# A new order of the work, a wider norm, a block placing moved to ScalarE and a last product moved to GpSimd in a two-layer hybrid model

## The reference

```python
def rms_norm(x, g):
    y = x * lax.rsqrt(jnp.mean(x * x, axis=-1, keepdims=True) + EPS)
    return y * g

for l in range(2):
    h = rms_norm(x, norm_mix_g[l])
    pa, pb, pc, pg = jnp.split(h @ w_in[l], GROUP_POINTS, axis=-1)
    oa = rwkv7_time_mix(pa, ...)          # S = S * w - (S kk)(kk a)^T + v k^T ; o = S r, token by token
    ob = stick_breaking_attention(pb)
    oc = differential_attention(pc, ...)
    ga, gb, gc = jnp.split(sigmoid(pg), 3, axis=-1)
    x = x + (ga * (oa @ w_branch_a[l]) + gb * (ob @ w_branch_b[l]) + gc * (oc @ w_branch_c[l])) @ w_out[l]
    x = x + conv_ffn(rms_norm(x, norm_ffn_g[l]), ...)
return rms_norm(x, norm_final_g)
```

## Time and profile before

| what | value |
|---|---|
| median of 3 runs | 1030.68 us (1030.68, 1030.68, 1032.37) |
| the profiled execution | 1032.37 us, of which the span is 1030.5 us and 1.9 us lie around it |
| PE, DVE, ACT, POOL busy | 98%, 80%, 60%, 1% |
| mean granted clock of TensorE | 0.997 |
| HBM | 157 GB/s, DMA engines 45% busy |

### The profile page before, as it was taken

How to read it: one execution, slowest core, us unless ns; L and a number is a source line. 1 busy time by engine, 2 the same in 40 slices (tenths; PEclk the granted TensorE clock), 3 DMA queues, 4 the chain that set the end, 5 groups by cost and what they waited for, 6 DMA issues and landing times.

```text
span 1030.5 us, 22708 instructions
## 1 busy us (share of the span) xinstructions
PE 1012.3 (98%) x8522; PEld 945.8 (92%) x8522; DVE 819.7 (80%) x1371; ACT 618.6 (60%) x967; POOL 11.9 (1%) x30
## 2 busy tenths in 40 slices
PE   8999999999999999999999999999999999999997
PEld 7998988899999999999999989789999999999996
DVE  6799763797797898878778996649968789887876
ACT  7964332656556665766689533246656666666765
POOL 0000000100000000000000000010000000000000
PEclk9999999999999999999999999999999999999999
DMA  8452342335445565555534533233435445555553
GB/s 300 156 173 103 116 150 64 114 111 177 156 157 182 181 206 184 185 190 180 197 131 155 175 111 135 83 90 126 148 141 184 165 164 204 193 192 190 184 185 126
DMA packets 46282, 163.93 MB, mean 159 GB/s; under 512 B 5904, under 2 KB 6080, under 8 KB 46192
## 3 DMA queue, kind: packets, MB, share of 16 engines
q1 hardware_dynamic: 44640, 160.19, 45.0%
q10 hardware_dynamic: 864, 1.63, 0.6%
q0 software_dynamic: 688, 0.81, 0.4%
HBM read 161.04 MB, written 1.05 MB: 157 GB/s over the span
## 4 chain that ended last, share of the span: by engine, by line
PE 85%; DVE 9%; ACT 3%; issue 2%; DMA 1%; SPq 0%; DVEq 0%; ACTq 0%
PE psum L468 84%; DVE sb_lo L1306 2%; ACT sb_rw L916 1%; DMA sb_raw<-w_stream 1%; DVE sb_inv L1555 1%; DVE sb_inv L1514 1%; DVE sb_inv L1517 1%; PE psum L786 1%; ACT sb_hh L916 1%; ACT sb_hi L916 0%; DVE sb_rw L1598 0%; DVE sb_yf L1579 0%; DVE sb_qb L1364 0%; DVE sb_rw L1485 0%; DVE sb_inv L1491 0%
## 5 line engine op out<-in xcount | busy, mean ns | idle before, releaser
L916 ACT ACTIVATE sb_hi<-sb_raw 128x1024 fp32r<-128x1024 f32 (+1 forms) x298 | 310.2, 1052 | 168.6 <-PE psum L468 158.6
L1306 DVE TENSOR_TENSOR sb_lo<-sb_raw,sb_hi 128x1024 fp32r<-128x1024 f32 x296 | 357.9, 1218 | 53.3 <-ACT sb_hi L916 52.9
L468 PE MATMUL psum<-sb_hh,sb_hi 128*128 128x256 f32 x1184 | 344.3, 291 | 2.6 <-DVE sb_lo L1306 1.3
L468 PE MATMUL psum<-sb_o,sb_hi 128*128 128x256 f32 (+1 forms) x1728 | 339.6, 308 | 1.3 <-DVE sb_o L1327 1.3
L468 PE MATMUL psum<-sb_hl,sb_hi 128*128 128x256 f32 x1184 | 335.5, 283 | 0.0
L468 PE MATMUL psum<-sb_hh,sb_lo 128*128 128x256 f32 x1184 | 335.2, 283 | 0.0
L468 PEld LDWEIGHTS psum<-sb_o,sb_hi 128*128 128x128 f32 x1728 | 278.6, 191 | 14.2 <-DVE sb_o L1327 1.7
L468 PE MATMUL psum<-sb_o,sb_lo 128*128 128x256 f32 x1056 | 243.8, 283 | 0.0
L468 PEld LDWEIGHTS psum<-sb_hh,sb_hi 128*128 128x128 f32 x1184 | 227.2, 192 | 17.2 <-issue 10.2
L468 PEld LDWEIGHTS psum<-sb_hl,sb_hi 128*128 128x128 f32 x1184 | 227.4, 192 | 0.7 <-issue 0.5
L468 PEld LDWEIGHTS psum<-sb_hh,sb_lo 128*128 128x128 f32 x1184 | 227.3, 192 | 0.0
(11 more groups left out here) (181 smaller groups left out, 938.0 us busy)
## 6 DMA issues: line engine op xcount, KB each, us to landing
sb_raw<-w_stream SPq DMA_DIRECT2D x299, 512.0 KB, 3.3
sb_pm<-mix_par ACTq DMA_DIRECT2D x2, 512.5 KB, 3.7
y_t<-sb_rw SPq DMA_DIRECT2D x4, 256.0 KB, 2.5
sb_cf<-const_f SPq DMA_DIRECT2D x1, 550.0 KB, 8.6
sb_pm<-mix_par SPq DMA_DIRECT2D x1, 512.5 KB, 9.8
sb_raw<-w_stream SPq DMA_DIRECT2D x2, 256.0 KB, 4.6
sb_x<-x_t ACTq DMA_DIRECT2D x2, 256.0 KB, 4.6
sb_x<-x_t SPq DMA_DIRECT2D x1, 512.0 KB, 6.1
```

What stands on the lines that cost most here:

```text
L468: return pe.matmul(out, lhsT, rhs, start=start, stop=stop, skip_group_check=True)
L916: return act.activation(out, in_, func, scale=scale, bias=bias, **kw)
L1306: tt(lo[:, s, :], raw[:, s, :], hi[:, s, :].bitcast(F32), ALU.subtract).then_inc(lo_done, 1)
```

## The change

Four things change.

1. The three orders are written anew. On TensorE, D27 now stands between `dxy` 16 and `m1` 32 of the first pair (before, between `m1` 32 and `dxy` 32), and D28 between `m1` 64 and `dxy` 64 (before, between `dxy` 32 and `m1` 64). Later D46 stands ahead of `btri` 0, D50 behind `btri` 2, D53 behind `cs` (0, 1), D59 between `cs` (2, 0) and `cs` (2, 1), D61 behind `cav` 2 together with D62. So `bav` 0 and `bz` 2, `bz` 3 and `btri` 2, `cs` (0, 0) and (0, 1), `cs` (3, 0) and (3, 1) become neighbours. The other entries keep their places on TensorE. On ScalarE and VectorE many splits and outputs change places among the steps; the set of them is the same.
2. VectorE's last addition of the two norms of a layer goes. TensorE sums two tiles instead of one, and both norms of a layer now have the products with one output column.
3. ScalarE copies all four strips of Y, VectorE none.
4. The last pair of tiles is multiplied on GpSimd, and SP's last store waits for that.

```diff
 STEPS = placed(
-    "+ D0-2 +3 D3-4 + D5 + D6 + D7-9 +4 D10-14 + D15-18 + D19 +3 D20 +2 D21 +5 D22-23 +3 D24 +2 D25-26 +6 D27 +2 "
-    "D28 +7 D29 +2 D30 +4 D31 +2 D32 +2 D33 +2 D34 +2 D35 +14 D36 +2 D37 +4 D38 +2 D39 +2 D40 + D41 + D42 + D43 "
-    "+2 D44-45 +2 D46 + D47 +2 D48-49 +3 D50 + D51 +3 D52 +3 D53 + D54 + D55 +2 D56 + D57 + D58 +4 D59-60 +2 D61 "
-    "+2 D62 + D63 + D64 + D65-67 + D68-71 + D72-81 + ")
+    "+ D0-2 +3 D3-4 + D5 +2 D6-9 +3 D10-11 + D12 + D13-18 + D19 +4 D20 +2 D21 +4 D22-23 +4 D24-25 + D26 +4 D27 +6 "
+    "D28 +5 D29 +2 D30 +4 D31 +2 D32 +2 D33 +2 D34 +2 D35 +14 D36 +2 D37 +4 D38 +2 D39 +2 D40 + D41 + D42 + D43 "
+    "+2 D44-46 + D47 +4 D48 + D49 +3 D50 + D51 +2 D52 +4 D53-54 + D55 +2 D56 + D57 + D58 +2 D59 +2 D60 +4 D61-62 "
+    "+ D63 + D64 + D65 + D66-68 + D69-81 + ")
...
-DVE_OWN = {"turn": 8, "layer": 125}
+DVE_OWN = {"turn": 8, "layer": 123}
...
             for b in range(4):
-                sp.wait_ge(y_ready, b + 1)
+                if b < 3:
+                    sp.wait_ge(y_ready, b + 1)
+                else:
+                    sp.wait_ge(y_last, 1)
                 sp.dma_start(y_out[:, 2 * b:2 * b + 2, :], HF[:, 2 * b:2 * b + 2, :]).then_inc(y_stored, 16)
...
+            pool.wait_ge(last_scaled, 2)
+            pool.wait_ge(rms_inv, 2 * DEPTH + 1)
+            pool.tensor_tensor(HF[:, 6:8, :], HF[:, 6:8, :], rs[:, 0:T].unsqueeze(1).broadcast_to([P, 2, T]), ALU.mult)\
+                .then_inc(y_last, 1)
...
             def norm(n):
                 pe.wait_ge(squared, n + 1)
-                last = mm(bank[4][:, 0:T], cst("ones"), XSQ[:, 0, :], True, n % 2 == 1)
-                if n % 2 == 0:
-
+                for c in range(2):
+                    mm(bank[4][:, 0:T], cst("ones"), XSQ[:, c, :], c == 0, False)
+                for c in range(2):
                     for tok in range(2):
-                        last = mm(bank[4][:, T + tok:T + tok + 1], XSQ[:, 0, tok * P:(tok + 1) * P],
-                                  cst("ones")[:, 0:1], False, True)
+                        last = mm(bank[4][:, T + tok:T + tok + 1], XSQ[:, c, tok * P:(tok + 1) * P],
+                                  cst("ones")[:, 0:1], False, c == 1)
                 last.then_inc(pe_["norm"], 1)
...
-                        pe.wait_ge(dve_mid["place"], n_of("place", l, c // 2 + 1))
...
-                    for v in range(2):
+                    for v in range(4):
                         ins = do(Y[:, :, :, BASE * v:BASE * (v + 1)],
...
-                norm(2 * l + 1, 4, T)
+                norm(2 * l + 1)
...
                 own.wait()
-                own.mark(tt(XSQ[:, 0:2, :], XSQ[:, 0:2, :], XSQ[:, 2:4, :], ALU.add))
-                own.wait()
-                tt(XSQ[:, 0, :], XSQ[:, 0, :], XSQ[:, 1, :], ALU.add).then_inc(squared, 1)
+                tt(XSQ[:, 0:2, :], XSQ[:, 0:2, :], XSQ[:, 2:4, :], ALU.add).then_inc(squared, 1)
...
-                    for v in (2, 3):
-                        ins = dve.tensor_scalar(Y[:, :, :, BASE * v:BASE * (v + 1)],
-                                                BOUT[1][:, :, 0, :].rearrange("p n (i z) -> p z i n", z=4)
-                                                [:, 2 * c:2 * c + 2], QUART[:, v:v + 1], None, ALU.mult)
-                    ins.then_inc(dve_mid["place"], 1)
...
-            for b in range(4):
+            for b in range(3):
                 pair = HF[:, 2 * b:2 * b + 2, :]
-                if b < 3:
-                    dve.wait_ge(scaled, 2 * b + 2)
-                else:
-                    dve.wait_ge(last_scaled, 2)
+                dve.wait_ge(scaled, 2 * b + 2)
                 tt(pair, pair, rep(rs[:, 0:T], 2), ALU.mult).then_inc(y_ready, 1)
```

More of the change, by code:

```diff
@@ L352, in hybrid_blocks @@
         merged_b, merged = sem("merged_b"), sem("merged")
-        y_ready, y_stored = sem("y_ready"), sem("y_stored")
+        y_ready, y_last, y_stored = sem("y_ready"), sem("y_last"), sem("y_stored")
         last_scaled, square_pairs = sem("last_scaled"), sem("square_pairs")
@@ L368, in hybrid_blocks @@
                              "ct", "cav", "blk")}
-        dve_mid = {k: sem("dve_mid_" + k) for k in ("lam", "prepb", "bon", "cs", "crms", "place")}
+        dve_mid = {k: sem("dve_mid_" + k) for k in ("lam", "prepb", "bon", "cs", "crms")}
         act_mid = {k: sem("act_mid_" + k) for k in ("up", "crms")}
@@ L1539, in step @@
                                       BXT.rearrange("p (q a r) -> p r a q", a=2, r=BASE)).then_inc(dve_["back"], 1)
-                        dve.wait_ge(dve_["back"], n_of("back", l, 1))
-                    else:
-                        dve.wait_ge(pe_["dxy"], n_of("dxy", l, ORD[("dxy", 1, LEVELS[-1])] + 1))
-                    for v in (2, 3):
-                        ins = dve.tensor_scalar(Y[:, :, :, BASE * v:BASE * (v + 1)],
-                                                BOUT[1][:, :, 0, :].rearrange("p n (i z) -> p z i n", z=4)
-                                                [:, 2 * c:2 * c + 2], QUART[:, v:v + 1], None, ALU.mult)
-                    ins.then_inc(dve_mid["place"], 1)
                 elif kind == "mat":
```

## The result

The changed kernel takes 1038.36 us (median of 6 runs, 1035.03 to 1038.71); the kernel before took 1030.83 beside it (6 runs, 1030.68 to 1032.69). The ratio is 1.0062, 95% interval 1.0050 to 1.0075: slower by 0.6%, where 0.34% was forecast. Ratios are worked out round by round and leave disturbed executions out, so that they can differ a little from the quotient of the medians. The profiled execution took 1038.57 us, of which 1036.8 are the span.

The account below looks back on a forecast made before the run. TensorE's queue, busy 98% of the span, was taken as the bound. From 1030.68 us, norms +3.3, placing +1.9, order -1.6, other orders 0 and last pair -0.1 gave +3.5: 1034.2 us, range 1031.8 to 1036.5.

Parts of the forecast that it names:

- The clock: Whole execution: the profile's one fall to 1.2 GHz lost 1.70 us; the median was taken as unfallen, so summed from 1030.68.
- rival (d): Clock falls in the usual execution too, at the new 1.5 us wait, two places, +1.7 each: 1035.9 to 1037.6; chance 0.13.
- Part 1: Both norms of each layer: more summing matmuls on TensorE cost +3.3 us (0.45 + 0.88 + 2.0); VectorE's dropped add gains nothing.
- rival (c): Norms: 22 narrow one-column matmuls follow in 0.03 us instead of 0.11, saving 1.8 us: 1032.4; chance 0.05.
- Part 2: Placing of the inverted blocks: four ScalarE copies in a row delay `dxy` by 0.93 us a layer, +1.9 in all.
- rival (b): Solver placing: VectorE's transpose comes 1.5 us earlier and hides the copies, giving 1031.2, no change; chance 0.08.
- (a): Both solver halves: VectorE's relief moves its results ahead and removes TensorE's waits, 3.4 us a layer, 1027.4; chance 0.04.
- Part 3: Order on TensorE: 0 in the solver's first half, later joined slabs save 0.8 us a layer, -1.6 in all.
- Part 4: Orders on ScalarE and VectorE: every split ready before its slab, tightest by about 0.9 us at slab 28; cost 0.
- rival (e): Orders on ScalarE and VectorE: a split comes late for a slab, +0.5 to +1.5 us a layer, 1035.2 to 1037.2; chance 0.10.
- Part 5: Last output pair on GpSimd: product takes 0.53 to 1.6 us, done before VectorE's third; -0.1 us, bounds -0.3 and +1.0.
- Rival (f): Kernel's end: GpSimd is late with the last output product, +1.1 us, giving 1035.3; chance 0.08.

Follow-up runs that it names:

- e12: The changed kernel timed again on another chip, nothing added: median 1038.28 us, ratio 1.0051 to the kernel before.
- e3: The changed kernel with strips 2 and 3 of Y copied by VectorE again: median 1037.60 us, ratio 1.0043 to the kernel before.
- e4: The kernel before with only the three new orders: median 1031.95 us, ratio 0.9992 to the kernel before.
- e5: The changed kernel with GpSimd's last product also waiting for VectorE's third product: median 1037.22 us, ratio 1.0046 to the kernel before.
- e8: The kernel before with the new orders only from D38 on: median 1031.34 us, ratio 0.9995 to the kernel before.
- e11: The kernel before with the new orders from D38 on and three unused fp32 matmuls between the layers: median 1032.34 us, ratio 0.9991.
- e13: The kernel before with eight unused fp32 matmuls of 256 columns between the layers: median 1035.18 us, ratio 1.0033.
- e9: The kernel before with four unused fp32 matmuls of 256 columns between the layers: median 1035.66 us, ratio 1.0016.
- e2: The changed kernel with VectorE's last add and the norms of the kernel before: median 1032.49 us, ratio 0.9999 to the kernel before.
- e6: The changed kernel with ten unused 128-column fp32 matmuls a layer in TensorE's waits in the solver's second half: median 1039.03 us, ratio 1.0065.
- e7: The kernel before with ten unused 128-column fp32 matmuls a layer in TensorE's waits in the solver's second half: median 1036.05 us, ratio 1.0038.
- e17: The changed kernel with the norms of the kernel before and four unused fp32 matmuls between the layers: median 1034.97 us, ratio 1.0027.

## Why the prediction was wrong, point by point

Right in direction, wrong in size: 1034.2 forecast, range to 1036.5, measured 1038.36. Executions without a fall are the ones that the sum spoke of: 1030.68 before, 1035.03 after, so +4.35 for a forecast of +3.5.

- **The clock, which is the step that failed.** "I take it that the median is this execution without the fall, and sum from 1030.68." For before, in its own batch, that came out right, and by luck: in the five other batches its median was 1.2 to 1.8 us higher, since about half of its executions had lost a fall's worth or more. (So in the batch of e12 the changed kernel is 5.8 us behind, not 7.5.) For after it was not asked again: the sum took full clock, and the falls were kept as rival (d) with 0.13. Two falls in the usual execution, as in the trace, or one of double length, as in that of e12, are 3.3 of the 4.2 us missed. (d) had the price right (1.6 measured, 1.7 given) and the number ("in two places"), and the place wrong: nothing falls behind the new wait of 1.3 us at `dxy` 16; they fall where before's one fall stood, in both layers. The sum should have asked how often that stretch falls, with layer 1 set 1.6 us later against layer 0, and not only whether it had changed.
- **Part 1, norms: +3.38 for +3.3.** Term by term 0.43, 0.87, 1.07, 1.01 for 0.45, 0.88, 1.0, 1.0. In layer 0 PE's wait before `up` hides half of the first norm, as said. All one-column records but the first pair are 0.11 us apart, as their weight loads are; rival (c) is out. The floor of 25 ns in the Trainium skill, "TensorE: Matmul & The Clock Gate", section "Wait — 56ns, not 53.3ns?", is a lower bound, and the trace does not contradict it; it is not the price here.
- **Missing from part 1:** that 22 more records ahead of layer 1's solver set it over the place where PE waits for its next instructions: +0.26.
- **Part 2, placing: +1.76 for +1.9.** `dxy` 2.48 behind `m1`, as said ("2.5 instead of 1.6"); rival (b) is out, and (a) too: VectorE's relief moved nothing.
- **Part 3, order: -2.32 for -1.6,** mis-sized. The merges in branches B and C are worth 1.16 a layer, not 0.8. The solver's 0 was right, but for a reason that I had not seen: e3 and e4 show that it hangs on the placing of part 2, and would be +0.5 a layer without it.
- **Part 4: 0, right;** rival (e) is out, behind the start of the execution no slab in the changed kernel waits longer for its split.
- **Part 5, the last product: +0.97 for -0.1.** Its bounds (-0.3, +1.0) held, the value did not. Two steps failed. "Between 0.53 and 1.6 us: done by 1026.6, before VectorE's third": it took 1.69 and, by itself, 1.26 (e5). And "the wait on POOL holds nothing else" looked at the queue alone: the product itself held VectorE's second one for 1.07 us. Rival (f) had the size (+1.1) by another road, GpSimd late; GpSimd was not late, it was done at 1032.07, and VectorE's third came at 1032.54 only because of it. And the value of +0.97 is not all holding: with GpSimd behind VectorE (e5) 0.43 of it stays. The Trainium skill, "SBUF — State Buffer", section "SBUF: two separate sides", has VectorE with two SBUF inputs and a GpSimd operation that reads SBUF share a port pair that one of them holds for a whole instruction while the other is blocked. The trace agrees nearly: GpSimd's product, begun at 1030.38 beside VectorE's first, takes 0.43 more than by itself, and VectorE's second, begun at 1030.86, ends 0.55 us behind GpSimd's, where a product that was blocked in full would take its own 0.69.

The sum with measured terms: 3.38 + 0.26 + 1.76 - 2.32 + 0.97 = +4.05; the other 0.3 of the 4.35 can lie in the start of the execution, which varies by more than that between traces (11.0 to 13.0 us from the first slab to the first norm); the execution of 1035.03 has no trace. Two falls make it +7.3, and 7.5 were measured.

What stays open: what makes a single layer of the changed kernel fall, and how much of it is the supply stall. No kernel here is faster than the one before with certainty: e4, e8 and e11, which have the new orders without the other parts, have ratios of 0.9992, 0.9995 and 0.9991, and all three intervals reach across 1.

## What to carry to other kernels

Where a trace shows one fall of the clock behind a stretch of small matmuls and waits, price the change twice, with as many falls as the stretch is repeated, and count as dangerous also what only moves such stretches against each other. Work for an idle engine is free only if what it reads and writes does not hold a busy one: put GpSimd's elementwise operation where VectorE is not working on two SBUF inputs and nothing waits for it, or leave it out. And undo the parts of a change together as well as singly: in the first half of the solver the new order alone costs 0.5 us a layer (e4), order and placing together 0.87, and the placing taken back alone returns only 0.35 (e3).

## What the runs showed of the hardware

- GpSimd's product of 128 x 512 fp32 with a broadcast operand: 1.26 us alone; beside VectorE's, 1.69, and VectorE's 1.75 instead of 0.69.
- Falls of the clock to 0.50 are 3.4 us long or twice that, cost 1.6 or about 3.2 us (e4, e5), and differ in number between executions of one kernel (1035.03 to 1038.71 us in six runs). The Trainium skill, "TensorE: Matmul & The Clock Gate", Part 1, has the activity monitor run free of the kernel's start, which would fit such scatter; that more added work can mean fewer falls (e13 against e9) would fit it too. No run here tests it.
- A stall of PE with nothing to wait for, 0.3 to 1.5 us, at a fixed number of records in the stream, which ends 2.2 to 2.5 us behind the start of a 16 KB instruction transfer. In layer 0 it is under 0.1 us in seven of the 20 traces (e2, e4, e6, e7, e8, e11, e17). The Trainium skill, "Runtime: NRT & Kernel Launch", section "Instruction fetch mechanics", has each sequencer fetch its instructions in blocks, mostly hidden; the trace shows the blocks, and here, among matmuls of 64 columns, the fetch was not hidden.
- A one-column fp32 matmul record costs 0.11 us when it has a weight load of 128 x 128 of its own.
- Four fp32 matmuls of 128 columns, put between matmuls of 64 columns, take 1.09 us, two take 0.64.
